# Two page tiles between the turned token tiles, and window keys turned before the last quarter of the pages

## The reference

```python
h = rmsnorm(x, norm_g[i])                      # the NSA norm, before layer 1's products
parts = split_cols(h @ w_in_nsa[l], NSA_SPLITS)
...
# samples: 16 pages of 128 tokens each, found through the page table
past_c = cache_cmp[page_table].reshape(Bd, PAST_LEN, 2, KV_HEADS, HEAD_DIM)
partials = jnp.concatenate([chunk_partials(past_c, cmp_pos_w), chunk_partials(kvc, cmp_pos_w)], axis=2)
kc_blk, vc_blk = blocks_from_partials(partials, cmp_phi)
...
s_c = q . kc_blk -> p_c, o_c, and from p_c the scores of 64-token blocks, of which the 16 best are kept
s_s = q . (selected keys) -> p_s, o_s          # raw pages of cache_sel
s_w = q . (last 512 tokens) -> p_w, o_w        # state_win_kv
out = gates[0] * o_c + gates[1] * o_s + gates[2] * o_w
```

## Time and profile before

| | us |
|---|---|
| median of 3 runs | 1127.64 (1126.96 to 1134.62) |
| profiled execution, device time | 1138.11 |
| span of the profile | 1136.4 |
| PE busy in the span | 1022.7 (90%) |
| mean granted clock of PE | 0.946 of full speed |

### The profile page before, as it was taken

The page is one execution under the profiler, slowest core; times in us unless marked ns, Lnnn a source line. Parts: engine busy times, 40 slices in busy tenths (PEclk is TensorE's granted clock), DMA queues, the critical chain, the costliest instruction groups (busy, mean ns, idle before and its releaser), DMA issues.

```text
span 1136.4 us, 17586 instructions
## 1 busy us (share of the span) xinstructions
PE 1022.7 (90%) x6558; PEld 627.7 (55%) x6558; DVE 589.0 (52%) x1326; ACT 309.2 (27%) x749; POOL 71.1 (6%) x124
## 2 busy tenths in 40 slices
PE   6999999999779994999999997778999798899897
PEld 3567677777544451577465465535555564565443
DVE  2207879776435636899000005247885465656113
ACT  4310000000420230111102115236776443543101
POOL 0000000000000000000000005120000112110000
PEclk9999999999969997999999987687999999999899
DMA  8623565453514366564221102430002857765202
GB/s 319 213 61 125 157 185 155 103 151 111 187 38 111 120 252 203 167 170 127 74 74 74 37 1 75 142 96 0 1 1 71 301 191 252 282 211 183 95 1 83
DMA packets 45727, 147.79 MB, mean 130 GB/s; under 512 B 8393, under 2 KB 20170, under 8 KB 38858
## 3 DMA queue, kind: packets, MB, share of 16 engines
q1 hardware_dynamic: 40522, 129.89, 36.2%
q0 software_dynamic: 5120, 16.78, 4.3%
HBM read 139.63 MB, written 15.27 MB: 136 GB/s over the span
## 4 chain that ended last, share of the span: by engine, by line
PE 69%; DVE 14%; DMA 6%; issue 5%; ACT 3%; SPq 1%; POOLq 1%; POOL 0%; DVEq 0%; ACTq 0%
PE PS L1179 60%; PE PS L1182 9%; DMA arena<-in_csel 3%; DVE arena L1811 2%; DVE arena L1812 2%; DVE arena L2077 1%; DMA arena<-in_cmem 1%; DMA arena<-in_ccmp 1%; DVE arena L2096 1%; DMA arena<-in_wall 1%; DVE arena L1814 1%; DVE arena L1901 1%; DVE arena L1781 1%; DVE arena L1891 1%; DVE arena L1820 1%
## 5 line engine op out<-in xcount | busy, mean ns | idle before, releaser
L1179 PE MATMUL PS<-arena 128*32 128x64 f32 (+16 forms) x5460 | 864.7, 384 | 48.2 <-DVE arena L1822 18.6
L1179 PEld LDWEIGHTS PS<-arena 128*128 128x128 f32 (+5 forms) x5460 | 497.7, 153 | 393.2 <-issue 258.1
L1182 PE MATMUL PS<-arena 128*128 128x128 f32 (+3 forms) x1098 | 174.5, 303 | 58.0 <-ACT arena L830 11.1
L1182 PEld LDWEIGHTS PS<-arena 128*128 128x128 f32 (+3 forms) x1098 | 131.2, 153 | 107.5 <-issue 48.0
L1811 DVE TENSOR_TENSOR arena<-arena 128x2048 f32<-128x2048 f32 x32 | 73.2, 2288 | 9.7 <-DMA arena<-in_ccmp 8.5
L1812 DVE TENSOR_TENSOR arena<-arena 128x2048 f32<-128x2048 f32 x32 | 73.1, 2285 | 0.0
L2007 DVE SCALAR_TENSOR_TENSOR arena<-arena 128x576 f32<-128x576 f32 x8 | 5.8, 757 | 127.7 <-ACT arena L1003 127.5
L1084 ACT ACTIVATE arena<-arena 128x512 f32<-128x512 f32 (+3 forms) x96 | 52.9, 554 | 22.8 <-DVE arena L2077 22.8
L2077 DVE CUSTOM_DVE_ANT_0 arena<-PS,arena 128x512 f32<-128x512 f32 (+3 forms) x96 | 41.3, 486 | 20.0 <-PE PS L1179 20.0
L535 POOL DMA_DIRECT2D arena<-in_csel x64 | 34.6, 541 | 240.7 <-PE PS L1182 112.1
L1970 DVE TENSOR_TENSOR arena<-arena,PS 128x512 f32<-128x512 f32 x16 | 11.0, 687 | 58.6 <-PE PS L1179 58.6
(11 more groups left out here) (182 smaller groups left out, 540.1 us busy)
## 6 DMA issues: line engine op xcount, KB each, us to landing
arena<-in_wall SPq DMA_DIRECT2D x20, 2048.0 KB, 9.4
arena<-in_ccmp SPq DMA_DIRECT2D x128, 256.0 KB, 3.9
arena<-in_csel SPq DMA_DIRECT2D x64, 256.0 KB, 5.6
arena<-in_csel POOLq DMA_DIRECT2D x64, 256.0 KB, 5.8
arena<-in_cmem SPq DMA_DIRECT2D x32, 256.0 KB, 3.9
arena<-in_win SPq DMA_DIRECT2D x8, 1024.0 KB, 9.6
out_win_s<-in_win SPq DMA_DIRECT2D x1, 8064.0 KB
arena<-in_xp SPq DMA_DIRECT2D x1, 2048.0 KB, 17.0
```

The lines of the kernel that those rows point to most:

```text
L1179: return nc.tensor.matmul(out, lhsT, rhs, start=start, stop=stop, skip_group_check=True)
L1182: return nc.tensor.transpose(out, in_, ident[0:in_.shape[0], 0:in_.shape[0]])
```

## The change

Two edits, each in the text of several engines.

On DVE, page tiles 20 and 21 are worked between `take_next(10)` and `take_next(11)`; before they followed `take_next(11)`. PE, ACT and SP keep their order there.

In sample attention the ten key steps of `front` take their sources in the order `TURNED`: steps 6 and 7 are the window, steps 8 and 9 the last quarter. Banks and copying engines still go by the step, so the window's first half is now copied by DVE (step 6), and both halves of the last quarter by ACT. PE's wait for the window's DMA stands before step 6, the wait for the last quarter's before step 8. The loads and their order are the same.

```diff
+TURNED = (0, 1, 2, 3, 4, 5, 8, 9, 6, 7)
...
@@ ACT, front: took
-                        if j < 8:
-                            nc.scalar.copy(skv(t.at(1), j // 2)[:, 2 * (j % 2):2 * (j % 2) + 2, 0:256],
+                        k = TURNED[j]
+                        if k < 8:
+                            nc.scalar.copy(skv(t.at(1), k // 2)[:, 2 * (k % 2):2 * (k % 2) + 2, 0:256],
                                            PS[:, 6 + j % 2, :].rearrange("p (q c) -> p q c", q=2)).then_inc(sa_fa, 1)
                         else:
-                            nc.scalar.copy(SWKT[:, j - 8, :], PS[:, 6 + j % 2, :]).then_inc(sa_fa, 1)
+                            nc.scalar.copy(SWKT[:, k - 8, :], PS[:, 6 + j % 2, :]).then_inc(sa_fa, 1)
...
@@ PE, front
                     else:
-                        if j == 8:
+                        if k == 8:
                             pe.wait_ge(sa_w[number % 3], 16 * (number // 3 + 1))
...
@@ DVE, after add_out(B_OUT0, 0)
-            for j in (9, 10, 11):
-                take_next(j)
-
-            for T in range(CONV_TILES + OUT0_TILES, PAGE_TILES):
+            take_next(9)
+            take_next(10)
+            page_tile(CONV_TILES + OUT0_TILES)
+            page_tile(CONV_TILES + OUT0_TILES + 1)
+            take_next(11)
+
+            for T in range(CONV_TILES + OUT0_TILES + 2, PAGE_TILES):
                 page_tile(T)
```

More of the change, by code:

```diff
@@ L1653, in front @@
                         pe.wait_ge(sa_fa if FRONT[j - 2] == "A" else sa_fd, front_value(t, j - 2))
[L1654 to L1658, removed]
+                    k = TURNED[j]
+                    if k < 8:
+                        if k % 2 == 0:
+                            places = 2 if k else 3
+                            pe.wait_ge(sa_lo[k // 2][number % places], 32 * (number // places + 1))
+                            pe.wait_ge(sa_hi[k // 2][number % places], 32 * (number // places + 1))
                         for q in range(2):
@@ L1661, in front @@
                                 ins = turn(PS[:, 6 + j % 2, 256 * q + 128 * g:256 * q + 128 * g + 128],
-                                           skv(number, j // 2)[:, 2 * (j % 2) + q, 128 * g:128 * g + 128])
+                                           skv(number, k // 2)[:, 2 * (k % 2) + q, 128 * g:128 * g + 128])
                     else:
-                        if j == 8:
+                        if k == 8:
                             pe.wait_ge(sa_w[number % 3], 16 * (number // 3 + 1))
                         for p in range(4):
-                            ins = turn(PS[:, 6 + j % 2, 128 * p:128 * p + 128], SWI[number % 3][:, p, 128 * (j - 8):128 * (j - 7)])
+                            ins = turn(PS[:, 6 + j % 2, 128 * p:128 * p + 128], SWI[number % 3][:, p, 128 * (k - 8):128 * (k - 7)])
                     ins.then_inc(sa_ft, 1)
@@ L2133, in took @@
                     dve.wait_ge(sa_ft, t.value(10, j + 1, base=START.sa_ft))
-                    tcopy(skv(t.at(1), j // 2)[:, 2 * (j % 2):2 * (j % 2) + 2, 0:256], PS[:, 6 + j % 2, :].rearrange("p (q c) -> p q c", q=2)
-                          ).then_inc(sa_fd, 1)
+                    k = TURNED[j]
+                    if k < 8:
+                        tcopy(skv(t.at(1), k // 2)[:, 2 * (k % 2):2 * (k % 2) + 2, 0:256],
+                              PS[:, 6 + j % 2, :].rearrange("p (q c) -> p q c", q=2)).then_inc(sa_fd, 1)
+                    else:
+                        tcopy(SWKT[:, k - 8, :], PS[:, 6 + j % 2, :]).then_inc(sa_fd, 1)
                 def cmp_max():
```

## The result

| | before | after |
|---|---|---|
| median of 19 runs each, taken beside each other, us | 1131.02 (1123.69 to 1138.47) | 1122.84 (1116.39 to 1127.05) |
| ratio after to before | | 0.9947 (95%: 0.9929 to 0.9965) |
| profiled execution, device time, us | 1138.11 | 1126.29 |
| span of the profile, us | 1136.4 | 1124.6 |
| mean granted clock of PE | 0.946 | 0.952 |

The change gains 0.53%, 6.0 us with an interval from 4.0 to 8.0 (the medians alone lie 8.2 apart). The forecast was a gain of 10.4 us. So stretches are compared from here on, and ratios.

What follows compares the result with a forecast made beforehand. PE was taken to bound the kernel nearly everywhere (69% of the span). Edit one's 5.7 and edit two's 4.7 us sum to 10.4, so 1127.64 - 10.4 = 1117 us, 0.9% faster; range 1110 to 1124, the forecast itself covering 1113 to 1121.

Steps and rivals of the forecast that it cites:

- Edit two, 4.7 us: Sample attention: window ahead of the last quarter removes most of six page waits totalling 7.2 us, gaining 4.7 us.
- the floor of 5.75 us: Sample attention: first values come 5.75 us after step 4 begins, 0.35 us above the 5.40 without the wait.
- the binding copy: Sample attention: ACT copies step 7 only after its 2.06 us exponential, and step 9 needs that bank.
- Rival (d): Sample attention: the exponential's place costs 1.2 us instead of 0.35, edit two does nothing; 1122 us, chance 0.09.
- the lower bound: Sample attention: edit two gains only 2 us if, among other reasons, unprofiled waits were smaller to begin with.
- Edit one, 5.7 us: Page tiles: 6.9 us from tile 22's earlier start, plus 1.37, less 2.6 for the clock, gained at 522.74.
- the 6.9 us for the landing of tile 22: Page tiles: tile 22 starts at 451, 6.9 us earlier; bounds 0 to 9.4 us earlier.
- From there DVE runs tile after tile without a gap: From tile 22's start to 522.74: only the landing of its pages sets the time, no later DVE waits.
- 1.37 - 2.6: PE after the new wait for tile 23: 1.37 us of slack, less 2.6 us lost to half clock.
- (a): Page tiles: tile 22's landing doesn't move, edit one loses about 1 us, edit two gains 4.7; 1124 us, chance 0.17.
- (b): Page tiles: pages land soon after issue, item 5 starts 12.1 us earlier, 16.8 with edit two; 1111 us, chance 0.12.
- (c): Restart after tile 23's wait: clock stays low, costing 6.8 less 1.37 us, landing unmoved; 1128.4 us, chance 0.03.

Runs made afterwards that it cites:

- e10: The kernel before, word for word, run for a second profile; its span is 1123.4 us.
- e1: The changed kernel with the old order of key steps, so edit one alone; ratio to before 0.9975 (2.8 us).
- e12: e3 with the old order of key steps, so copy late and edit one alone; ratio to before 0.9826.
- e9: The changed kernel with the copy of key step 7 moved from ACT to DVE; ratio to before 0.9941.
- e2: The changed kernel with DVE's old order of page tiles, so edit two alone; ratio to before 0.9943 (6.4 us).
- e4: e3 with DVE's old order of page tiles, so copy late and edit two alone; ratio to before 0.9945.
- e7: The changed kernel with 13 more products on PE behind item 5, results unused, to keep it busy; one run, 1121.86 us.
- e3: The changed kernel with the copy of 8064 KB issued later, behind the first memory loads of layer 1; ratio to before 0.9786.
- e6: The changed kernel with tile 26's pages issued ahead of block 2's weights; one run, 1121.61 us.

## Why the prediction was right or wrong

**Edit two, 4.7 us: right.** The wait for the pages fell to 0.3, the floor of 5.75 us is 5.79, the binding copy is the one named. The samples' pace gives about 4.6 us; the ratios give 3.2 to 6.4, with wide intervals. Rival (d) is excluded: its floor would have been 0.85 us higher. What the wait was "to begin with" changes from one execution to the next (7.2 in before, 6.3 in e10, 4.6 in e1, 7.8 in e12), as the lower bound had allowed for, so the closeness of 4.7 is in part luck.

**Edit one, 5.7 us: mis-sized, and this is the step that failed.** The mechanism was the one described: SP issues at 422.85, DVE waits for pages, PE for tile 23, with a half clock in and behind the wait. The runs give 2 to 3 us where 5.7 stood. Two terms failed, the 6.9 us for the landing of tile 22 and the nothing that was set for later waits of DVE. Term by term:

- "6.9 us earlier" was 5.75 in after's own profile and 3.3 on average over three profiles in the old order and six in the new. The prediction let tile 22 start 16.9 us behind the copy's end before (441 to 457.92) and 10.0 behind it now. (Its 448.9 is a slip of the sum, 441 + 7.6 is 448.6, and of no weight beside the 2 us added.) By the copy's packets it ended at 442.3 in before, and tile 22 starts 15.1 to 15.7 us behind the copy's end in the old order (mean 15.3) and 10.7 to 11.9 in the new (mean 11.5): 1.6 us less at the one end, 1.5 at the other, and the copy itself ends 0.5 us later in the stretch. The rest behind the copy was let go at 206 GB/s; the weights did (222), the pages went at 127. This 127 at a share of 0.48 stood in the earlier trace rows. Why a half of the engines moves pages more slowly than weights was not looked into. The bounds of this term, 0 to 9.4, held.
- "From there DVE runs tile after tile without a gap" was true of the one trace of before, where tile 26, behind 2 MB of weights, came within the 11.0 us that it had (issued at 479.35, wanted at 490.3). In after the same loads took 13.8 us (472.94 to 486.73). After has a wait of 2.94 there, e1 2.38, e9 2.31; so has e2 in the old order (2.30); e10, e4 and e7 have none. With the copy and these loads in place that is one of three profiles in the old order and three of four in the new. Whether the new order makes the wait likelier or this is chance is open. With DVE's pace alone, and PE at full clock, a gain would have stood to the end. Here 2.8 of the 5.75 us went at tile 26, and 5.75 - 2.8 = 2.9 is what the stretch shows (89.15 - 86.27).
- "1.37 - 2.6" for the clock, a loss of 1.2, was nearly right for PE's own path (1.4 by the rows above) but did not count. The wait at tile 26 made DVE later still, so PE lost nothing by being slow, and its 1.4 us of waiting at tile 29 stayed. The two losses do not add up: the larger counts.

**The sum.** With the measured terms, 2.9 for edit one in this profile (2 on average) and about 4.6 for edit two make 6.6 to 7.5, inside the interval of 4.0 to 8.0. In after's own profile both conditions of the forecast came true, tile 22 between 449 and 454 and edit two at 3 to 6, and still its 1113 to 1121 does not hold the median of 1122.84; there the loss lies between tile 22 and the end of the stretch. With the average landing, tile 22 would be at 454.6. The wide range (1110 to 1124) holds the median, though these runs' before is at 1131.02 and not at 1127.64, so the ratio is the fairer measure: 1127.64 x 0.9947 = 1121.7. Of the rivals (d) gave the nearest number, 1122, by a mechanism that is excluded. (a) was half right in its mechanism: the landing of tile 22 did move, but on average by less than half of the 6.9 us. (b) failed because each load waits for its busy half, as said against it; the packets show just that. (c) did not happen.

## What to carry to other kernels

When the trace shows one wait and you cure it, list every load that stands behind the same long transfer, and every one that came "just in time" in the one trace you have: the next wait is among them. Here a DMA share near one half beside a queue of issued loads meant that one transfer kept half of the engines to itself. Look for that, and reshape such a transfer or move it first: two cures that gave 2 and 0 to 1.4 us singly gave 18 to 21 together (18 by the ratios of e3 and e2, 21 by the stretch, 88.8 against 67.83).

## What the hardware showed that was not expected

- A DRAM-to-DRAM copy of 8064 KB with an outer dimension of 8 moved at 206 GB/s with a share of 0.48; with 16 outer pieces the engines were at 0.99 and 317 to 344 GB/s, nearly all of it the copy's own, and it took 25.7 us instead of 40.2. A load of 2 MB issued behind the first took 39.6 to 45.2 us to land, and 8.2 us with the copy away (e3).
- With half of the engines at work (share 0.51) the weights moved at 222 GB/s and the raw pages at 127.
- A half clock was free where another engine set the pace: PE lost 2.8 us to it in after and 1.7 in e6, and the stretch 0 and 0.3.
- Two executions of the same kernel differ by 13 us in span (1136.4 in before and 1123.4 in e10) and by 1.5 us in the wait for tile 22; the wait for tile 26 came and went between executions (none to 2.94 us). One profile gave the mechanisms; for sizes of a few microseconds it took several.
